# A decoder step: the sample's attention and the prompt's projection put into one stage

## The reference, cut to what matters

```python
proj = _rmsnorm(x, g) @ w                      # 1024 -> 3072: q, k, v of "sb", q, k, v of "dil"
# prompt: _sb_prompt, _dilated_prompt over its own 1024 tokens
# sample: stick-breaking over 4096 paged cache positions and the new ones,
#         dilated windows over a cache of 2048 positions and the new ones
o_a = _sb_sample(qa, ka, va, k_past, v_past, sb_bias[l])
o_b = _dilated_sample(qb, k_buf, v_buf, rel_bias)
xs = _finish(xs, o_a, o_b, ...)                # output projection, residual, MLP, as for the prompt
```

## Time and profile before

| | us |
|---|---|
| median of 3 runs | 2215.3 (2209.49 to 2215.92) |
| profiled execution, its own time | 2211.82 |
| its span, first to last instruction | 2210.0 |
| mean granted clock of TensorE, share of full speed | 0.905 |
| bytes moved by DMA | 373.89 MB |
| busy: PE, DVE, ACT, POOL | 1801.2, 936.0, 556.4, 531.8 |

### The profile page before, as it was taken

One profiled execution on the slowest core, in us unless ns is written; L12 is line 12 of the kernel. 1 busy time (PEld: TensorE's weight loads), 2 busy tenths in 40 slices (PEclk: granted clock), 3 DMA queues, 4 the chain that ended last, 5 costly groups with the idle time before them and its releaser, 6 DMA issues. The chain is left out here.

```text
span 2210.0 us, 37863 instructions
## 1 busy us (share of the span) xinstructions
PE 1801.2 (81%) x16830; PEld 1590.4 (72%) x16834; DVE 936.0 (42%) x857; ACT 556.4 (25%) x908; POOL 531.8 (24%) x377
## 2 busy tenths in 40 slices
PE   4999997487887825665666579699999999999997
PEld 4999995265655613333333469699999999999997
DVE  5310112477776639766765274722212212122223
ACT  4100101466667402221322310321121212111122
POOL 3111200000000025665665410321112112211210
PEclk7999996699999957878888789799999999999999
DMA  6222317711200059999999820433433333343332
GB/s 220 79 89 78 107 44 287 252 39 39 77 11 10 26 159 414 419 422 422 421 420 408 326 83 1 152 114 133 153 114 131 134 132 114 128 156 114 114 131 92
DMA packets 118370, 373.89 MB, mean 169 GB/s; under 512 B 18121, under 2 KB 59593, under 8 KB 106185
## 3 DMA queue, kind: packets, MB, share of 16 engines
q0 software_dynamic: 40192, 251.94, 29.0%
q1 hardware_dynamic: 74712, 117.92, 15.4%
q10 hardware_dynamic: 3360, 2.47, 0.4%
HBM read 336.58 MB, written 102.57 MB: 199 GB/s over the span
## 5 line engine op out<-in xcount | busy, mean ns | idle before, releaser
L404 POOL TENSOR_TENSOR mlp_w_lo<-mlp_raw,mlp_w_hi 128x2048 fp32r<-128x2048 f32 x30 | 138.1, 4603 | 587.9 <-ACT mlp_w_hi L450 587.9
L1285 PE MATMUL sa_s<-sa_kT,sa_qd 128*32 128x256 f32 x1344 | 129.0, 550 | 155.6 <-DVE sa_kT L1549 97.1
L1285 PEld LDWEIGHTS sa_s<-sa_kT,sa_qd 128*32 128x32 f32 x1344 | 52.5, 146 | 213.3 <-DVE sa_kT L1549 104.7
L563 DVE TENSOR_TENSOR xT<-xT,mlp_acc 128x1088 f32<-128x1088 f32 x64 | 82.4, 1287 | 280.0 <-PE mlp_acc L145 280.0
L145 PE MATMUL mlp_acc<-n_hi,mlp_w_hi 128*128 128x272 f32 x1024 | 172.1, 290 | 20.7 <-POOL mlp_w_lo L121 16.3
L1549 DVE STREAM_TRANSPOSE sa_kT<-sa_k_in 128x2048 f32<-128x2048 f32 x64 | 147.1, 2306 | 78.5 <-DMA sa_k_in<-in_cache_sb_k,sa_k_rows 75.5
L145 PE MATMUL mlp_acc<-mlp_h_hi,mlp_w_hi 128*128 128x272 f32 x1024 | 170.7, 288 | 3.9 <-DVE mlp_h_lo L559 3.9
L145 PE MATMUL mlp_acc<-n_hi,mlp_w_lo 128*128 128x272 f32 x1024 | 171.2, 289 | 0.0
L145 PE MATMUL mlp_acc<-n_lo,mlp_w_hi 128*128 128x272 f32 x1024 | 171.2, 289 | 0.0
L145 PE MATMUL mlp_acc<-mlp_h_lo,mlp_w_hi 128*128 128x272 f32 x1024 | 169.9, 288 | 0.0
L145 PE MATMUL mlp_acc<-mlp_h_hi,mlp_w_lo 128*128 128x272 f32 x1024 | 169.9, 288 | 0.0
(11 more groups left out here) (178 smaller groups left out, 3168.9 us busy)
## 6 DMA issues: line engine op xcount, KB each, us to landing
out<-in_cache_win_k POOLq DMA_DIRECT2D x16, 2040.0 KB, 8.8
out<-in_cache_win_v POOLq DMA_DIRECT2D x16, 2040.0 KB, 8.8
mlp_raw<-in_w_up SPq DMA_DIRECT2D x16, 1024.0 KB, 11.8
mlp_raw<-in_w_down SPq DMA_DIRECT2D x16, 1024.0 KB, 11.7
qkvT<-qkv_out SPq DMA_DIRECT2D x24, 544.0 KB, 2.7
qkv_raw<-in_w_in SPq DMA_DIRECT2D x12, 1024.0 KB, 5.4
na_rows_in<-qkvT SPq DMA_DIRECT2D x16, 544.0 KB, 7.0
out<-na_nat POOLq DMA_DIRECT2D x4, 2048.0 KB, 10.8
```

Source lines behind the costliest of these rows:

```text
L404: pool.tensor_tensor(out=ring.lo[:, n % 2, :], in0=ring.raw[:, n % 2, :], in1=ring.hi[:, n % 2, :].bitcast(F32), op=ALU.subtract).then_inc ...
L563: dve.tensor_tensor(in_banks(xT[:, c, :]), in_banks(xT[:, c, :]), acc[:, c % 2, :, 0:BW], ALU.add).then_inc(added, 1)
L1285: last_one = pe.matmul(out[h * 32:(h + 1) * 32, :], qd[:, k, x, :], keys[:, x, :], start=(b == 0), stop=(b == 1 and stop))
```

## The change

There are two new stages in place of `gains_stage`, `load_tokens`, the first `dense_stage` and `sample_stage`.

`first_stage` loads and turns the tokens, the sample's tile first, prepares `hi`, `lo` and `root` for the 1024 tokens of the prompt, makes the table `by_distance` and the bias for the sample's dilated units, and projects the 64 tokens of the sample alone: 12 steps, each with 1 MB of `w_in` (two chunks of 128 columns), in plain fp32 with the tokens as the stationary operand. All of `w_in` (12.6 MB) is read here once, and again in the next stage.

`projection_and_sample_stage` runs over 47 steps. The prompt's projection is cut into 48 banks, one for each 128 columns of `w_in` and each 512 tokens; a bank is 24 matmuls of 512 columns. Banks 0 to 3 stand in step 0, and one more in each step up to 44. The same steps hold the sample's 42 units. Their buffers are smaller: three slots for 1 MB of keys, two for turned keys of half a unit each (so `score` now waits, multiplies and signals once for each half, in matmuls of 128 columns), and five for 512 KB of values, a quarter of a unit. The weights are turned in the step of `turn_step(n)`, three after the score for most, two units in one step at steps 6, 7 and 9 of each group, and the values are multiplied one step later. The sample's new queries and keys no longer come from `qkvT`; SP loads them in rows into `nat` and VectorE turns them there.

`natural_stage` no longer handles the sample or the table and has three PSUM buffers where it had two. The host lays `w_in` out so that a chunk of 128 columns is contiguous, 4 KB to a partition.

```diff
+    tiles = [(SEQ, NS)] + [(t * P, P) for t in range(QT)]
+    NX, NW = 4, 3
...
+    pairs = [(4, 3), (1, 0), (5, 2)]
+    steps = [(j, u) for j in range(3) for u in range(W // P)]
...
+                def load_weights(i):
+                    j, u = steps[i]
+                    if i >= NW:
+                        sp.wait_ge(projected, i - NW + 1)
+                    for x, g in enumerate(pairs[j]):
+                        sp.dma_start(w[:, i % NW, x, :], w_in[g * (W // P) + u]).then_inc(w_loaded[i % NW], 16)
...
+                for i in range(len(steps)):
+                    load_weights(i)
+                    if i == 5:
+                        sp.wait_ge(left_out, len(tiles))
+                        sp.wait_ge(right_out, len(tiles))
+                        sp.dma_start(xT_kept.rearrange("(c p) t -> p c t", p=P), xT[:, :, :]).then_inc(kept, 16)
+                    if i in (8, 11):
+                        store_projection((8, 11).index(i))
+                store_projection(2)
...
+                def project(i):
+                    j, u = steps[i]
+                    pe.wait_ge(w_loaded[i % NW], 32 * (i // NW) + 32)
+                    cols = slice(u * P, (u + 1) * P)
+                    for k in range(KC):
+                        for x in range(2):
+                            back = x == 1 and pairs[j][x] in (0, 3)
+                            last = pe.matmul(acc[x * NS:(x + 1) * NS, j, cols], xs[:, k, back * NS:(back + 1) * NS],
+                                             w[:, i % NW, x, k * P:(k + 1) * P], start=(k == 0), stop=(k == KC - 1))
+                    last.then_inc(projected, 1)
...
+                for i in range(4):
+                    project(i)
+                for c in range(KC):
+                    pe.wait_ge(squared, c + 1)
+                    for b in range(SEQ // QB):
+                        last = pe.matmul(turned[:, 0, b * QB:(b + 1) * QB], ones[:, :], square[:, c % 2, b * QB:(b + 1) * QB],
+                                         start=(c == 0), stop=(c == KC - 1))
+                    last.then_inc(added, 1)
+                for i in range(4, len(steps)):
...
+                load_bias(0)
+                act.wait_ge(gain_loaded, 16 * len(gains))
+                for c in range(KC):
+                    if c == 0:
+                        act.wait_ge(left_out, len(tiles))
+                    if c == half:
+                        act.wait_ge(right_out, len(tiles))
+                    act.activation(hi[:, c, :], xT[:, c, 0:SEQ], ACT.Copy, scale=gains[0][0][:, c:c + 1]).then_inc(hi_done, 1)
+                    if c >= 2:
+                        act.wait_ge(added, c - 1)
...
+                    act.activation(out_s[:, j, :], acc[:, j, :], ACT.Copy, scale=inv_s[:, at:at + 1]).then_inc(projection_out, 1)
...
+        turned = st.enter_context(nc.psum_tensor("na_turned", [P, 3, 2, 512], F32))
...
-    LAG = 6
-    KS, VS, WS = 4, 3, 7
+    KS, KT, VS, WS = 3, 2, 5, 4
     NL = ND * KW + G * TS
+    BANKS = SEQ // QB
+    NZ = CHUNKS * BANKS
+    AHEAD = 4
...
+    def turn_step(n):
+        m = n % NU
+        return n // NU * NU + (6, 6, 7, 7, 8, 9)[m] if m <= ND else n + 3
+    STEPS = turn_step(N - 1) + 3
+    def turned_in(s):
+        return [n for n in range(N) if turn_step(n) == s]
+    banks = [[] for _ in range(STEPS)]
+    for z in range(NZ):
+        banks[max(0, z - AHEAD + 1)].append(z)
     use = {}
-    for p in range(2):
...
+                def load_new_rows(i):
+                    p, x = i // 2, i % 2
+                    g, k = p // 2, p % 2
+                    if i:
+                        sp.wait_ge(prepared, i)
+                    sp.wait_ge(nat_cleared, 1)
+                    for a in range(G):
+                        b = g * G + a
+                        src = new_rows[k][0][b].rearrange("t h d -> t (h d)") if x else q_back[k, b * TS:(b + 1) * TS, :]
+                        sp.dma_start(nat[a * 40:a * 40 + TS, :], src).then_inc(nat_loaded, 16)
                 def load_new(e):
...
+                for s in range(STEPS):
+                    for z in banks[s]:
+                        if z % BANKS == 0 and 2 <= z // BANKS + 1 < CHUNKS:
+                            load_weights(z // BANKS + 1)
+                        store_bank(z)
...
+                def low(c):
+                    pool.wait_ge(hi_done, c + 1)
+                    pool.tensor_tensor(out=wl[:, c % 2, :], in0=wr[:, :], in1=wh[:, c % 2, :].bitcast(F32), op=ALU.subtract)\
+                        .then_inc(lo_done, 1)
+                def load_keys(x):
+                    n, q = x // 2, x % 2
+                    if x >= KS:
+                        pool.wait_ge(kT_done, x - KS + 1)
+                    g, m = n // NU, n % NU
...
+                def load_values(y):
+                    n, a = y // G, y % G
+                    if y >= VS:
+                        pool.wait_ge(valued, y - VS + 1)
...
+                for x in range(KS):
+                    load_keys(x)
+                low(0)
+                low(1)
+                for x in range(KS, KS + 2):
+                    load_keys(x)
+                for y in range(VS):
+                    load_values(y)
+                for s in range(STEPS):
+                    for x in range(2 * s + KS + 2, 2 * s + KS + 4):
+                        if x < 2 * N:
+                            load_keys(x)
+                    for z in banks[s]:
+                        if z % BANKS == BANKS - 1 and 2 <= z // BANKS + 1 < CHUNKS:
+                            low(z // BANKS + 1)
+                    for n in turned_in(s - 1):
+                        for y in range(G * n + VS, G * n + VS + G):
+                            if y < G * N:
+                                load_values(y)
...
+                def bank(z):
+                    c, b = z // BANKS, z % BANKS
+                    pe.wait_ge(lo_done, c + 1)
+                    if z >= 3:
+                        pe.wait_ge(acc_out, z - 2)
+                    w_hi, w_lo = (x[:, c % 2, :].rearrange("p (k n) -> p k n", k=KC) for x in (wh, wl))
+                    cols = slice(b * QB, (b + 1) * QB)
+                    for k in range(KC):
+                        for part, (w, x) in enumerate(((w_hi, hi), (w_hi, lo), (w_lo, hi))):
+                            last_one = pe.matmul(acc[:, z % 3, :], w[:, k, :], x[:, k, cols], start=(k == 0 and part == 0),
+                                                 stop=(k == KC - 1 and part == 2))
+                    last_one.then_inc(acc_done, 1)
...
+                    for q in range(2):
+                        pe.wait_ge(kT_done, 2 * n + q + 1)
+                        for f in range(2):
+                            out = s_ps[:, n % 2, f * KW:(f + 1) * KW]
+                            if k == SB:
+                                out = out[:, q * P:(q + 1) * P]
+                            else:
+                                out = out.rearrange("p (j q c) -> p q j c", j=2, q=2)[:, q, :, :]
+                            last_one = products(out, kT[:, (2 * n + q) % KT, :, :], k, f, True)
+                        last_one.then_inc(scored, 1)
...
+                for s in range(STEPS):
+                    for n in turned_in(s - 2):
+                        if last(n):
+                            place(n)
+                    for z in banks[s][:-1]:
+                        bank(z)
                     if s < N:
                         score(s)
-                    if 0 <= no < N and last(no):
-                        place(no)
-                    if 0 <= n < N:
+                    for z in banks[s][-1:]:
+                        bank(z)
+                    for n in turned_in(s - 1):
+                        if first(n):
+                            values_new(n)
+                        values(n)
+                    for n in turned_in(s):
...
+                def evict(z):
+                    dve.wait_ge(acc_done, z + 1)
+                    if z >= 2:
+                        dve.wait_ge(bank_stored[z % 2], 16 * (z // 2))
+                    b = z % BANKS
+                    dve.tensor_tensor(out[:, z % 2, :], acc[:, z % 3, :], root[:, b * QB:(b + 1) * QB], ALU.mult).then_inc(acc_out, 1)
...
+                evict(0)
                 turn_keys(0)
-                dve.wait_ge(bias_in, 16 * (2 * G + 3))
-                for s in range(N + LAG + 2):
-                    no = s - LAG - 2
-                    if 0 <= no < N and last(no):
-                        own_heads(no)
...
+                    for z in banks[s][-1:]:
+                        evict(z)
+                    for n in turned_in(s - 1):
+                        if last(n):
+                            own_heads(n)
...
+            projection_and_sample_stage(nc, cx, a["w_in"], hi, lo, root, qkvT, oT_dram, a["sb_bias"],
+                                        (a["cache_sb_k"], a["cache_sb_v"]), (a["cache_win_k"], a["cache_win_v"]), q_back,
```

(7 more changed lines are left out.)

645 lines of the change are left out of this document (346 added, 299 removed).

## The result

The changed kernel takes 2122.5 us (median of 4 runs, 2117.5 to 2126.4) where the one before took 2215.6 in the same session: ratio 0.958, 95% interval 0.955 to 0.961. The gain is 93 us; 189 were forecast, and 2122.5 lies above the range (1985 to 2100). Its profiled execution has a span of 2118.1 us.

A forecast was written before the change was run, and what follows sets the result against it. DMA at 421 GB/s was taken to bound the combined stage's full steps. First stage 82, combined stage 557, natural and prompt stage 421 and the rest 964 gave a span of 2024, so 2026 us; range 1985 to 2100.

The forecast's parts named there:

- the full steps: Combined stage, 24 steps with score, bank and one unit of values: DMA sets them, 11.8 us each, 283 us.
- rival 1: Everything hides in the combined stage: full steps 11.2 us, no stalls in double steps, total 1983 us; chance 0.10.
- the bank: Combined stage, TensorE: 24 matmuls of 512 columns at 0.225 us each, 5.4 us.
- the sums of squares: First stage, TensorE between projection steps 3 and 4: 32 instructions of 512 columns, 15 us.
- the terms of the untouched stages: Natural and prompt stage 421 us, all behind it 964 us.
- Rivals 3 and 4: 3: TensorE at its lower clock, 2304 us, chance 0.03. 4: no overlap, banks add to the sample's 479, about 2207, 0.02.
- rival 2: Combined stage: slower transfers (12.8 us a step, 2058) or loads landing in 10 us (13.9, 2096); chance 0.22.
- the term of the double steps: Steps 7 to 10 of each group, seven units of values on five quarter-slots: 64 us, with three stalls of about 4.
- steps 0 to 6: Start of the combined stage, score and bank only, no values: 7.5 us each, 52 us.
- steps 23 and 24: Combined stage, counted among the 24 full steps at 11.8 us each.
- steps 25 to 27: Combined stage, steps without values between the two groups' values: 23 us.
- the term of the first stage: Stage ends at 82 us, bounds 72 to 95: sums run to about 57, then five weight loads of about 3.5 each.

The follow-up runs named there:

- e1: Changed kernel with a step's first unit of weights turned on TensorE at the step's start, not behind the values: 2106.7 us, 0.951 of the kernel before.
- e2: Changed kernel with the second group's two loads of new rows issued and turned in separate steps: 2106.6 us, 0.951 of the kernel before.
- e5: Changed kernel with e1's edit and values spread by quarters, five or four in each step: 2067.8 us, 0.935 of the kernel before.
- e15: Changed kernel with six slots for quarters of values, not five, half the dilated bias table left out: 2109.9 us, 0.952 of the kernel before.
- e3: Changed kernel with SyncE issuing second new rows and chunk 2's weights earlier at the combined stage's start: 2111.3 us, 0.954 of the kernel before.
- e9: Changed kernel with the edits of e5, e2 and e3 together, first stage unchanged: 2052.2 us, 0.927 of the kernel before.
- e7: Changed kernel with a fourth slot for weights in the first stage: 2112.6 us, 0.954 of the kernel before; stage to 104.0 us.
- e4: Changed kernel with both halves of the first stage's bias loaded at about 35 us: 2118.9 us, 0.9565 of the kernel before.
- e10: Changed kernel with the edits of e7 and e4 together: 2112.0 us, 0.954 of the kernel before; first stage to 101.5 us.
- e12: Changed kernel with e7's slot and the kept tokens' store three weight steps later: 2108.7 us, 0.952 of the kernel before; stage to 104.0 us.
- e13: Changed kernel with e10's edits and the kept tokens stored from ScalarE's queue: 2112.5 us, 0.954 of the kernel before; stage to 103.3 us.

## Why the prediction was wrong in size

**Right.** The direction; that DMA sets the full steps, at 413 GB/s, forecast 11.8 us apart and measured 11.4 over steps 11 to 22 and 11.2 over steps 32 to 40 (rival 1's length); the bank (5.7 us; 5.4 forecast, since a matmul of 512 columns follows after 0.232 us, not 0.225); the eviction (0.68 us); the sums of squares (15.4 us; 15); the terms of the untouched stages. VectorE and GpSimd do collide, the product L1843 takes 3.02 us beside a split and 0.69 alone, and in full steps it is covered, as priced. The Trainium skill ("GPSIMD Engine Reference", "Key points") names instructions with two inputs in SBUF among those that suffer. The rows agree with that: three evictions (at 172.3, 437.9 and 466.9 us), with one input in PSUM, lay wholly beneath a split and took 0.69 us, where all 48 took 0.68 in the mean. Rivals 3 and 4 did not come, nor rival 1 as a whole; the measured time lies above rival 2's end (2096), for another reason than rival 2 gave: loads and slots were fast enough wherever the work was even.

**Wrong: the term of the double steps** ("4 x 7.3 + 7 x 2.8 + 3 x 4 = 61 ... I take 64"). The mechanism, five quarter-slots for eight quarters, was right. The size was off: 96.4 and 89 us, 57 more in all, the largest part of the miss. "About 4 us each" priced one wait. In step 8 it is 5.3 + 1.7 + 1.0 us; the score, the late quarters and the turns run at the lower level, 3 us more; and as score, key turns and key loads depend on each other, nothing else advances. Part of it, in steps 9 and 30, 12 us by their lengths in e1, has another cause, which the prediction lacks: the fall from seven to four slots of gate results. And 6 us of step 7 are the small loads of e2. With the quarters spread the catch-up of a group takes 24 and 23 us less (e5); without e1's part that leaves 35 us in all, which shows the bunching as the main cause; e15 shows that the way of the first late load weighs more than the number of slots.

**Wrong: steps 0 to 6** (68 us; 52 and some 4 of the softmax were forecast). Step 1 alone took 9 us too long (16.8, not 7.5), behind a split that waited for its weights by SyncE's order (e3). The prediction had reckoned with GpSimd's order in full steps, not at the start. But e3 brought steps 0 to 6 down by 4 us only, since step 2 grew: what holds the first steps then stays open.

**Wrong: steps 23 and 24** (15.1 and 15.9 us, taken as 11.8 each). Small loads again; e2 took 6 us off them. It was luck that the sum of the full steps came out all the same: the others were 0.4 to 0.6 us shorter than forecast in the mean, and the 23 lengths that can be read add up to 269 us, against 271.

The other terms of the stage nearly cancel: the start took 30.5 us (28), steps 25 to 27 29.5 (23, and some 4 of the softmax), and what follows the last score 45.8 (47).

The causes mended together gave 70.3 us (e9), about the excess of the stage (628.5 against 557). That the two figures agree is partly chance, since even quarters also remove time that the forecast had allowed.

**Wrong: the term of the first stage** (82 us, bounds 72 to 95). Half of the 27 us lies ahead of the sums' end: 70.5 us, not 57, with tokens that end at 32, sums of the sample's squares of 4 us on TensorE which the sum left out, and 6.7 us for late weights. The other half lies behind: from 57 on "the remaining five then pace the end at about 3.5 us each" made 17.5 us, while TensorE started on the last load only at 102.6. The reason given, three slots that halt the loads, is worth 4.8 us (e7), the slow bias loads 3.5 (e4), the two together 7.3 (e10), the order or queue of the kept tokens nothing that shows in the stage's end (e12, e13): whichever transfer is moved, another load becomes the late one. These figures come from one profile each, and singly only the slot's gain is clear of noise in the medians (9.9 us). The window has 231 GB/s over the stage, some 25 MB, where I had counted with 321. What else would bring the rate up stays open; leaving the kept tokens out was not tried.

## What to carry to other kernels

Where a ring of slots holds a little more than one step's loads, spread the consumption to what the ring holds before counting the slots; a step that takes more than the ring pays the whole way of a load, and everything tied to its engine stands still. When a stage is made longer by fewer slots, list each ring that shrank and, for each, who waits in the same step; then do the same for the first two steps, where every in-order queue still carries its setup. Check a sum for the saturated stretch and for the stretches around it separately: here the length of a saturated step was right within 5%, and nearly all of the miss lay around it. And read what an edit frees at the next step too: what e3 took from step 1 came back in large part in step 2.

## What the runs showed of the hardware

- Two loads, each of four transfers of 8 rows of 2 KB, cost VectorE 3.6 and 2.6 us of waiting in the middle of a saturated stage, and one of them 11.5 us at the start, where weights had been issued ahead of it (the row below).

```profile
128.39 0.71 DVE L1762 STREAM_TRANSPOSE sa_kT_new<-sa_nat 128x512 f32<-128x512 f32 x1 [11.54 <-DMA sa_nat<-out]
```

- Four loads of 257 KB, rows of 8 KB that start 4 bytes apart, took until 91 us when issued at 70.6; the weights behind them landed after 17 us, against 8.3 in the median. From 76 to 90 us DMA was busy 0.94 and moved 244 GB/s.
- DMA held 413 GB/s over 92 us of gathers, direct loads and stores together. The Trainium skill ("DMA: Bandwidth & Descriptors", "Where 436 GB/s comes from") has the HBM side bind at about 358 GB/s for a core, half of what it gives for the two cores of a stack. Here, with one core at work, it did not bind; the measurement decides.
